# Two experts at fixed ranks, their weights in front of the ranking, and another order of weight pieces and places

## The reference

```python
def _moe(h, w_router_l, bias_l, w_gate_l, w_up_l, w_down_l, w_sh_gate_l, w_sh_up_l, w_sh_down_l):
    scores = jax.nn.sigmoid((xt @ w_router_l).astype(jnp.float32))
    biased = scores + bias_l.astype(jnp.float32)
    ...
    sel = lax.top_k(cand, TOP_K)[1]
    wts = jnp.take_along_axis(scores, sel, axis=1)
    ...
    def expert_block(args):
        xe, e = args
        return (jax.nn.silu(xe @ w_gate_l[e]) * (xe @ w_up_l[e])) @ w_down_l[e]
    ...
    shared = (jax.nn.silu(xt @ w_sh_gate_l) * (xt @ w_sh_up_l)) @ w_sh_down_l
    return (routed + shared).reshape(b, l, d)
```

## Time and profile before

| | |
|---|---|
| median of 3 runs | 2994.2 us (2988.68 to 2994.72) |
| the profiled execution | 2992.89 us, span 2991.1 us |
| TensorE busy (matmul) | 2436.7 us, 81% of the span |
| VectorE busy | 1598.9 us, 53% |
| ScalarE busy, GpSimd busy | 836.0 us, 830.9 us |
| moved by DMA | 885.95 MB, mean 296 GB/s |
| mean granted clock of TensorE | 0.918 |

### The profile page before, as it was taken

The page is one execution under the profiler, slowest core; times in us unless marked ns, Lnnn a source line. Parts: engine busy times, 40 slices in busy tenths (PEclk is TensorE's granted clock), DMA queues, the critical chain, the costliest instruction groups (busy, mean ns, idle before and its releaser), DMA issues.

```text
span 2991.1 us, 29479 instructions
## 1 busy us (share of the span) xinstructions
PE 2436.7 (81%) x9692; PEld 1331.3 (45%) x9692; DVE 1598.9 (53%) x3289; ACT 836.0 (28%) x2272; POOL 830.9 (28%) x723
## 2 busy tenths in 40 slices
PE   7898888888887988998897899789797786767673
PEld 3684333333333766344443455458783532222221
DVE  4556657485444636758889877556644521121111
ACT  1313333333332412343343444323110111111110
POOL 1004333343331102334444556112010112122221
PEclk9799999999999799999999999899998788888887
DMA  7029999999998126999898899612113399999994
GB/s 276 1 85 403 422 422 422 422 415 422 422 398 346 57 85 248 376 366 395 355 420 313 358 422 395 245 43 71 43 57 131 140 408 397 389 391 381 382 381 147
DMA packets 129843, 885.95 MB, mean 296 GB/s; under 512 B 23184, under 2 KB 23568, under 8 KB 31760
## 3 DMA queue, kind: packets, MB, share of 16 engines
q0 software_dynamic: 86976, 553.74, 46.0%
q1 hardware_dynamic: 42704, 330.22, 27.5%
HBM read 877.56 MB, written 37.75 MB: 306 GB/s over the span
## 4 chain that ended last, share of the span: by engine, by line
PE 46%; DMA 25%; DVE 20%; ACT 4%; issue 3%; SPq 1%; POOL 1%; DVEq 0%; ACTq 0%; POOLq 0%
PE ps L155 44%; DMA ring<-in_peer_uv,idx_u 11%; DMA ring<-in_w_gu 6%; DVE ring L1307 6%; DVE arena L76 5%; DMA ring<-in_w_down 3%; ACT arena L125 3%; PE ps L158 2%; DMA arena<-in_w_gu 2%; DMA arena<-in_w_down 1%; DVE arena L1307 1%; DVE iu L113 1%; DVE arena L109 1%; SPq L2560 1%; DVE arena L97 1%
## 5 line engine op out<-in xcount | busy, mean ns | idle before, releaser
L155 PE MATMUL ps<-ring,arena 128*128 128x512 f32 (+3 forms) x3264 | 1262.9, 653 | 281.2 <-ACT arena L125 159.9
L155 PEld LDWEIGHTS ps<-ring,arena 128*128 128x128 f32 (+2 forms) x3264 | 473.6, 180 | 957.3 <-issue 605.1
L1307 DVE CUSTOM_DVE_ANT_0 ring<-ring,h 128x1024 f32<-128x1024 f32 x448 | 563.0, 1257 | 328.3 <-DMA ring<-in_peer_uv,idx_u 294.9
L2377 POOL DMA_INDIRECT ring<-in_peer_uv,idx_u x448 | 491.5, 1097 | 754.8 <-PE ps L155 609.4
L155 PE MATMUL ps<-arena 128*128 128x128 f32 (+7 forms) x2504 | 502.8, 383 | 106.4 <-ACT arena L125 42.9
L125 ACT ACTIVATE arena<-arena 128x1 f32<-128x1 f32 (+4 forms) x1097 | 296.7, 270 | 747.6 <-DVE arena L1307 646.3
L155 PEld LDWEIGHTS ps<-arena 128*128 128x128 f32 (+3 forms) x2504 | 316.0, 193 | 263.5 <-issue 148.3
L76 DVE TENSOR_TENSOR arena<-arena,ps 128x512 f32<-128x512 f32 (+1 forms) x158 | 93.7, 593 | 446.9 <-ACT arena L125 358.6
L125 ACT ACTIVATE arena<-ps 128x512 f32<-128x512 f32 (+4 forms) x198 | 109.8, 554 | 774.1 <-PE ps L155 712.5
L155 PE MATMUL ps<-ring,hT 128*128 128x512 f32 (+2 forms) x896 | 307.0, 503 | 16.9 <-DVE hT L97 11.9
L125 ACT ACTIVATE arena<-cst,arena 128x128 f32<-128x128 f32 x512 | 205.5, 401 | 162.3 <-PE ps L155 122.0
(11 more groups left out here) (117 smaller groups left out, 1486.6 us busy)
## 6 DMA issues: line engine op xcount, KB each, us to landing
ring<-in_w_gu SPq DMA_DIRECT2D x98, 1024.0 KB, 28.5
ring<-in_w_down SPq DMA_DIRECT2D x52, 1024.0 KB, 29.8
ring<-in_w_in SPq DMA_DIRECT2D x16, 2048.0 KB, 12.6
arena<-in_w_gu SPq DMA_DIRECT2D x30, 1024.0 KB
ring<-in_w_mod SPq DMA_DIRECT2D x12, 2048.0 KB
ring<-in_peer_wq SPq DMA_DIRECT2D x8, 2048.0 KB, 8.1
ring<-in_w_o SPq DMA_DIRECT2D x6, 2048.0 KB, 11.1
ring<-in_w_gates SPq DMA_DIRECT2D x12, 1024.0 KB, 4.9
```

Source lines behind the costliest of these rows:

```text
L155: return self.e.matmul(o, lhsT, rhs, start=start, stop=stop, skip_group_check=True)
L1307: v.done(v.e.tensor_tensor_reduce(out=row, in0=row, in1=h[:, n // 128, :], scale=1.0, scalar=0.0, op0=ALU.mult, op1=ALU.add, accum_out=aa[ ...
L2377: g.e.indirect_dma_start(out=landing(n), out_offset=None, in_=d["peer_uv"], in_offset=bass.IndirectOffsetOnAxis(ap=idx_u[:, n:n + 1], axis ...
```

## The change

Experts 0 and 1 get ranks 8 and 9, whatever their size. VectorE takes their keys out before the sort (copy to `kp`, fill with -1), and puts them back, raised by 65536 and 32768, after the first eight have been found; the raised part is a multiple of 64 and falls out of the digits. The capacity bounds move: ranks 0 to 7 up to 128, 8 to 31 up to 64 with the check at rank 10 and a check of its own for the two, ranks from 32 up to 32. The second wave's list has two positions more, for ranks (10, 11) beside (8, 9) and for a second round of ranks 32 to 35. The pieces of ranks 8 and 9 are addressed by constants, so SyncE waits for the order only ahead of the first piece of another rank. The down pieces of step 0 stand directly behind its gate and up pieces, as numbers 4 and 5; so 6 to 13 are gate and up of step 1, and from 14 on the numbers are as before. Places 8 to 12 are other pieces of memory: 8 is where the router's bias was, 9 to 11 are in the arena, 12 is where the shared expert's down weights were. The shared expert's store to `y_tab` stands ahead of piece 13, no longer ahead of piece 9.

```diff
--- before.py
+++ after.py
@@ -256,18 +256,24 @@
 
 
 STEPS = expert_steps()
-CAPACITIES = ((0, 128), (8, 64), (32, 32))
-AGAIN = [(r,) for r in range(32)] + [(8, 9)] + [tuple(range(32 + 4 * i, 36 + 4 * i)) for i in range(8)]
-AGAIN_FROM = [128] * 8 + [64] * 24 + [192] + [32] * 8
+KNOWN = {8: 0, 9: 1}
+CAPACITIES = ((0, 128), (10, 64), (32, 32))
+AGAIN = [(r,) for r in range(32)] + [(8, 9), (10, 11)] + \
+    [tuple(range(32 + 4 * i, 36 + 4 * i)) for i in range(8)] + [(32, 33, 34, 35)]
+AGAIN_FROM = [128] * 8 + [64] * 24 + [192] * 2 + [32] * 8 + [64]
 WAVES = (STEPS, AGAIN)
 FIRST = [[sum(len(x) for x in steps[:s]) for s in range(len(steps))] for steps in WAVES]
 LAST_CHUNK = 6
 PLACES = 13
 
 
 PIECES = [[(t, part, i) for s in range(len(steps) + 1) for t, part in ((s, 0), (s, 1), (s - 1, 2))
            if 0 <= t < len(steps) for i in range(len(steps[t]))] for steps in WAVES]
+PIECES[0] = PIECES[0][0:4] + [(0, 2, 0), (0, 2, 1)] + [x for x in PIECES[0][4:] if x[0:2] != (0, 2)]
 PIECE_OF = [{x: n for n, x in enumerate(pieces)} for pieces in PIECES]
 
 
@@ -292,7 +298,7 @@
         self.hsh = ar(15104, 512)
         self.sums = [two(6400, 2048), two(8448, 2048)]
         self.sh2 = modT[:, 24:32]
-        self.row_of, self.add_to = iu[:, 0:64], iu[:, 64:132]
+        self.row_of, self.add_to = iu[:, 0:64], iu[:, 64:136]
         self.digits, self.expert = iu[:, 192:256], iu[:, 256:320]
 
 
@@ -405,7 +411,7 @@
         def piece(wave, *which):
 
             i = PIECE_OF[wave][which] % PLACES
-            return R(2 * i, 2) if i < 10 else ar(16384 + 2048 * (i - 10), 2048)
+            return R(2 * i, 2) if i < 8 else R(18, 2) if i == 8 else ar(16384 + 2048 * (i - 9), 2048) if i < 12 else R(16, 2)
 
         def gate_place(j):
             return R(13 + 2 * (j % 2), 2)
@@ -1739,8 +1745,13 @@
                           ("out", "rank", c))
                     v.ts(m.RW[:, c, 0:64], m.RW[:, c, 0:64], 1000.0, None, ALU.add, None, ("RW", c))
                 v.stt(m.key, tile_of("sizes")[:, 0:64], 64.0, m.rev, ALU.mult, ALU.add, ("out", "sizes"))
+                v.cp(m.kp[:, 0:2], m.key[:, 0:2])
+                v.fill(m.key[:, 0:2], -1.0)
                 for i in range(8):
                     o8 = m.order[:, 8 * i:8 * i + 8]
+                    if i == 1:
+                        for e in range(2):
+                            v.ts(m.key[:, e:e + 1], m.kp[:, e:e + 1], 32768.0 * (2 - e), None, ALU.add, None)
                     v.max8(o8, m.key)
                     if i < 7:
                         v.replace8(m.key, o8, m.key, -1.0)
@@ -1752,7 +1763,9 @@
                 v.ts(m.Pm, m.rank, m.colm, None, ALU.is_equal, None, ("permutation",))
                 for i, (rank, n) in enumerate(CAPACITIES):
                     v.ts(m.ssum[:, i:i + 1], m.order[:, rank:rank + 1], 64.0 * (n + 1), None, ALU.is_ge, None)
-                for i in (1, 2):
+                v.tt(m.ssum[:, 3:4], m.kp[:, 0:1], m.kp[:, 1:2], ALU.max)
+                v.ts(m.ssum[:, 3:4], m.ssum[:, 3:4], 64.0 * 65, None, ALU.is_ge, None)
+                for i in (1, 2, 3):
                     v.tt(m.ssum[:, 0:1], m.ssum[:, 0:1], m.ssum[:, i:i + 1], ALU.max)
                 v.cp(flag[:, 0:1], m.ssum[:, 0:1], ("over",))
                 v.wait_ge(*at("ps", "by rank", 0))
@@ -1813,11 +1826,11 @@
                             o = m.OH[:, c, k % 8, :].rearrange("p (x s) -> p x s", x=by)
                             v.tt(o, bc(C("iota")[:, first:first + P // by], 1, by),
                                  bc(m.rkp[:, c, rs[0]:rs[0] + by], 2, P // by), ALU.is_equal, ("onehot", 1, k))
-                    ig = rows(1, 0, 0, 41)
+                    ig = rows(1, 0, 0, 43)
                     v.cp(m.iy[:, 0:32], ig[:, 0:32])
-                    v.tt(m.iy[:, 32:34], sr[:, 0:2], ig[:, 32:33].to_broadcast([P, 2]), ALU.add)
-                    v.tt(heads(m.iy[:, 34:66], 8), bc(ig[:, 33:41], 2, 4), bc(sr[:, 2:6], 1, 8), ALU.add)
-                    v.cp(m.add_to[:, 0:66], m.iy[:, 0:66], ("slots", 1, 0))
+                    v.tt(heads(m.iy[:, 32:36], 2), bc(ig[:, 32:34], 2, 2), bc(sr[:, 0:2], 1, 2), ALU.add)
+                    v.tt(heads(m.iy[:, 36:72], 9), bc(ig[:, 34:43], 2, 4), bc(sr[:, 2:6], 1, 9), ALU.add)
+                    v.cp(m.add_to[:, 0:72], m.iy[:, 0:72], ("slots", 1, 0))
 
                 def experts(wave, more):
                     steps = WAVES[wave]
@@ -2651,26 +2664,31 @@
 
             def weights(wave, before):
 
-                sp.wait_ge(*at("order"))
                 e = {}
                 for n, (s, part, i) in enumerate(PIECES[wave]):
-                    if wave == 0 and n == 9:
+                    if wave == 0 and n == PLACES:
                         load(rows_of(y_tab[0:T, :]), m.ysh, s_tab, ("tables",),
                              after=[("out", "ysh", c, i) for c in range(2) for i in range(2)])
                     rank = WAVES[wave][s][i]
                     if wave == 0 and n == 20:
                         load(hT_sb[:, 0:D], d["rows"][14:15, :].to_broadcast([P, D]), s_post, ("loaded", "ffn", "post"),
                              after=[("ps", "shared", 1)])
-                    if part == 0:
+                    known = wave == 0 and rank in KNOWN
+                    if known:
+                        which = slice(KNOWN[rank], KNOWN[rank] + 1)
+                    elif part == 0:
+                        sp.wait_ge(*at("order"))
                         e[rank] = sp.e.value_load(m.expert[0:1, rank:rank + 1], min_val=0, max_val=63) if at.known else 0
-                    src = d["w_down"][bass.ds(e.pop(rank), 1), :, :] if part == 2 else \
-                        d["w_gu"][bass.ds(e[rank], 1), :, 2048 * part:2048 * part + 2048]
+                    if not known:
+                        which = bass.ds(e[rank] if part < 2 else e.pop(rank), 1)
+                    src = d["w_down"][which, :, :] if part == 2 else d["w_gu"][which, :, 2048 * part:2048 * part + 2048]
                     old = [("used", "piece", wave, *PIECES[wave][n - PLACES][0:2])] if n >= PLACES else before(n)
                     load(piece(wave, s, part, i), src.rearrange("a p n -> (a p) n"), piece_sems[wave][n % PLACES],
                          ("loaded", "piece", wave, s, part, i), after=old)
 
             weights(0, lambda n: [("used", "mo", 1)] if n < 3 else [("used", "mo", 0)] if n < 6 else
-                    [("ps", "shared", 1)] if n < 8 else [("used", "w_sh"), ("used", "router bias")] if n < 10 else [("x stored",)])
+                    [("ps", "shared", 1)] if n < 8 else [("used", "router bias")] if n == 8 else
+                    [("x stored",), ("zeros stored",)] if n < 12 else [("used", "w_sh")])
             sp.wait_ge(*at("over"))
             for x in range(2):
                 sp.wait_ge(*at("first wave", x))
```

## The result

The changed kernel takes 3006.1 us (median of 5 runs, 3004.4 to 3010.5) against 2990.0 us (5 runs, 2988.7 to 2994.7) for the kernel before. The ratio is 1.0048, with a 95% interval of 1.0037 to 1.006: some 14 us slower, where 8.4 us were forecast. The two medians lie 16.1 us apart and the two profiled executions 12.6 us; where I say 14 us, it is by the ratio. The profiled execution of the changed kernel took 3005.5 us, its span is 3003.4 us, 12.3 us longer than the span before.

What follows compares the result with a forecast made beforehand. Weight bytes bound the body, after a head at TensorE's pace. A 2.88 MB deficit (7.1 us, including 0.9 us of head delay) plus 1.3 us restart gave 8.4 us: 2992.9 + 8.4 = 3001.3 us, range 2990 to 3006 us.

Steps and rivals of the forecast that it cites:

- What bounds the kernel: Expert stage: TensorE sets the pace in the head, weight bytes in the body, at 2.58 us per piece.
- The early pieces: Before the order: six weight pieces load from about 2342 to 2362 us, up to 15.5 us of DMA work moved forward.
- The added wait: SyncE's queue: pieces 17 and 18 wait 27 us for step 0's down product, leaving a DMA hole of some 20 us.
- The size of the sum: At the restart weights are 2.88 MB behind, 7.1 us, plus 1.3 us for restarting: 8.4 us slower.
- Worse: Rival: step 0's down product slips by more than 3 us, time over 3006 us; chance 0.02.
- The first term: TensorE's head moves 0.9 us later, bounds 0.5 to 1.4 us; the clock was given 3 us either way.
- VectorE's part: Added VectorE work: 0.7 us before the order and 0.2 us left after it, 0.9 us in all.
- The second term: After the restart: a full DMA makes up the deficit at 406 GB/s, with gathers equal in both kernels.
- that rival: Later body: slack in the DMA dips from 2640 to 2900 us absorbs the lag, about 2993 to 2996 us; chance 0.11.
- The rival of the head start: SyncE's queue: piece 17 goes out behind the first half of up of step 1, giving 2986.7 us; chance 0.10.
- The break-even that I gave: SyncE's queue: the kernel is faster if piece 17 is issued before 2422.6 us.
- The second wave: After the first wave: no expert exceeds its capacity, so it isn't run; if run, about 3550 us, chance 0.01.

## Why the prediction was right, and where it was off

*What bounds the kernel:* right. In the body the rates and shares are those of before, and the lag that the head leaves, 14.9 us at up of step 4, is there at the end but for 1.3 us.

*The early pieces:* right. They go out at 2340.7 us, move at 427 GB/s from 2346 to 2360 us, and then, from 2362 to 2370 us, the DMA is at 1 GB/s. They are worth nothing in the changed kernel, as the run with the order waited for first shows. The Trainium skill (DMA: Bandwidth & Descriptors, Rules for kernel authors) advises to issue a DMA early and to wait on its semaphore late, because the fixed setup cost then overlaps. What was moved in front here is 15.5 us of transfer and not setup alone, and the runs show it to pay only in the kernels in which the places behind it come free in time.

*The added wait:* right, in its place, its length (27 us forecast, 27.9 measured) and what is queued behind it. That it is the cause is shown by the run with the line alone in the kernel before (1.0041), the one with the line taken out (0.9989) and the one with places by use (0.9989).

*The size of the sum was wrong:* 8.4 us were forecast, some 14 us came. The 3006.1 us lie at the very edge of my range and above the 2998 to 3005 us that I gave the forecast itself. By a little it is the case that I called *Worse*, chance 0.02: a down product that slips by more than 3 us, here 3.5, and a time over 3006 us. Two terms were too small. The first term is the head. I let it move by 0.9 us and gave the clock 3 us either way. VectorE's part was right: from the `x_tab` store to the order it is 32.2 us for 31.4, and the shared down product begins at 45.3 us for 44.3. But the down product of step 0 ends 93.7 us after the store for 90.2, 3.5 us later. Between, the same work takes longer: the shared down product 9.88 us for 8.68, and ahead of up of step 1 the one-hot products 1.70 for 1.12 and the transposes 2.40 for 1.31. Up of step 1 itself doesn't, 9.72 us for 9.85. The granted clock shows it. Busy time in the shared down product, 48 to 51 us after the `x_tab` store in both, and in those one-hot products and transposes, first of the changed kernel, then of the kernel before:

```profile
2386.44:2389.44 3.00, 3.00 (x5) 1.34 (x4) 0.69 (x1) 0.00 (x0) 1.19 (x2) 0.53 1.00 376
...
2406.10:2410.00 3.90, 3.90 (x42) 3.55 (x42) 1.17 (x4) 0.32 (x1) 0.00 (x0) 0.53 1.01 429
```

```profile
2387.75:2390.75 3.00, 3.00 (x8) 1.33 (x7) 0.51 (x1) 0.60 (x1) 0.46 (x1) 1.00 1.02 418
...
2405.10:2407.40 2.30, 2.29 (x42) 2.11 (x42) 0.54 (x2) 0.11 (x1) 0.00 (x0) 1.00 0.98 415
```

From 48 us after the store the kernel before has 1.00, 2.4 GHz, and the changed one still 0.53, near 1.2 GHz. The one-hot products and transposes run at 1.00 in the kernel before and at 0.53 in the changed one. The seven profiles with the fixed ranks all have the shared down product at 9.66 to 9.88 us; the three without them have 8.60 to 8.71. So the head's end is 3.5 us late where I had 0.9, and the forecast becomes 8.4 + 2.6 = 11.0 us. The 2.6 us were within my bounds for the clock, but I took the middle and they fell at the edge.

The second term had no bounds at all: after the restart, the stretch to the second half of up of step 4 takes 54.3 us where it took 50.6. DMA by queue between 2433.5 us, the restart, and 2487.8 us, and for the kernel before the same work, 2423.7 to 2474.3 us:

```profile
q1 hardware_dynamic: 2676, 19.01, 85.2%
q0 software_dynamic: 1440, 2.19, 15.8%
```

```profile
q1 hardware_dynamic: 2642, 18.70, 88.7%
q0 software_dynamic: 1147, 1.64, 13.1%
```

GpSimd moves 2.19 MB in it and not 1.64, and SyncE's queue 0.31 MB more; at 391 GB/s 0.86 MB are 2.2 us of the 3.7. The rest is the rate, 391 against 403 GB/s. My sum had put both at nothing: it took the rate of the full head for the deficit and no GpSimd work to be made up. Why the rate is lower wasn't tried. The piece that TensorE waits for there, the chain of the changed kernel as in the earlier trace rows:

```profile
2452.91 34.83 DMA ring<-in_w_gu
```

It lands at 2487.7 us, against the store 14.9 us later than in the kernel before; I had said 8.4. One sign of mine failed: TensorE was to wait for no weight before 2460 us, and it does, in up of step 3, where the kernel before doesn't:

```profile
2453.13 5.35 PE L155 MATMUL ps<-ring,arena 128*64 128x512 f32 x16 [2.46 <-DMA ring<-in_w_gu]
```

The body, in which TensorE waits for bytes, so begins a step sooner than I had it. At the end 13.6 us of the 14.9 are left, so the lag isn't absorbed later, and that rival falls, but for 1 us.

*The rival of the head start* would have had 2986.7 us. The run with places by use is that rival made true, and it has 2991.1, a ratio of 0.9989: piece 17 leaves 3.5 us later against the store than in the kernel before, where I had let it 0.9, since the head is late. The break-even that I gave, piece 17 at 2422.6 us or 82.9 us after the store, holds well: it leaves 3.6 us sooner than that, at 79.3 us, and the kernel is 3 us faster.

*The second wave* is not run.

## What to carry to other kernels

With a ring of buffers and one in-order issuing engine, count for each load which use it waits for, and give a new load the place that is freed next by use, not the one that was filled next; moving two transfers forward in the list moved a wait to the wrong product and cost 12 us by itself. An early load is worth at most what the places behind it let through: with six pieces of 15.5 us in front of 13 places the whole change brought 3 us, and 6 us when the consumer's head was made sooner. A forecast for a head that one engine sets has to carry that engine's clock as a term of its own.

## What the runs showed of the hardware that I had not expected

A small delay of TensorE can come with a larger one by its clock. In the six profiles that have the seven added VectorE operations, 1.0 us on the path, and not the moved products, the down product of step 0 ends 93.6 to 93.8 us after the store, 3.5 us later than before. The shared down product runs longer at 1.2 GHz before the clock rises, and the one-hot products and transposes ahead of up of step 1, which ran at 2.4 GHz, run at 1.2 GHz. That it is the clock is read from the granted clock's rows; that the delay is what shifts the clock against the work was only argued. In the seventh, with the shared products moved, the head ends at 90.2 us, as before, though its shared down product takes 9.86 us too. In the kernel before with the moved VectorE products it goes the same way: a 3.3 us wait of TensorE is followed by a product of 9.84 us for 7.09, at a granted clock of 0.50 from 2401 to 2406 us.

The gathered rows that TensorE waits for there were issued while the weights issued from 2377 us were still landing, and the first gather landed 9.25 us after its issue. In the kernel with places by use and the same edit, with six pieces in place already, those of step 0 took 6.2 us each. That the queue makes the difference wasn't tried by itself.
